# Attention scores of a hybrid decoder layer from split queries and keys, halves stacked over the 128 rows

## What is computed

```
qg = q.reshape(*lead, tq, N_KV_HEADS, GROUP, HEAD_DIM)
s = jnp.einsum('...qkgd,...skd->...kgqs', qg, k) * (HEAD_DIM ** -0.5)
s = jnp.where(valid, s + bias, -jnp.inf)
p = softmax of s with a sink logit per head
o = jnp.einsum('...kgqs,...skd->...qkgd', p, v)
...
z = h @ w_in        # queries, keys, values, gates, convolution inputs
y_conv = (cb * short_conv(u_ext, conv_w)) @ w_conv_out
mix = sigmoid(ga) * y_conv + sigmoid(gb) * (o @ w_attn_out)
x = x + mix @ w_o;  x = x + hier_moe(rms_norm(x))
```

## Time and profile before

| | us |
|---|---|
| median of 3 runs (lowest, highest) | 1737.24 (1736.86, 1740.86) |
| the profiled execution: its time | 1738.65 |
| its span from the first to the last instruction | 1737.1 |

### The profile page before, as it was taken

How to read it: one execution, slowest core, us unless ns; L and a number is a source line. 1 busy time by engine, 2 the same in 40 slices (tenths; PEclk the granted TensorE clock), 3 DMA queues, 4 the chain that set the end, 5 groups by cost and what they waited for, 6 DMA issues and landing times. The chain is left out here.

```text
span 1737.1 us, 26183 instructions
## 1 busy us (share of the span) xinstructions
PE 1653.6 (95%) x9527; PEld 1474.4 (85%) x9527; DVE 1036.5 (60%) x1839; ACT 834.0 (48%) x1202; POOL 234.0 (13%) x197
## 2 busy tenths in 40 slices
PE   5999999999999999999999999699999999999991
PEld 4899899999999999999999888478888888877871
DVE  5322466656556432114222576788989899888883
ACT  5000355555555430113112211378788888877773
POOL 1100000000000100000000111322322323222310
PEclk9999999999999999999999999799999999999996
DMA  6242111111111301114113711799999999999956
GB/s 161 79 125 86 40 41 46 49 36 36 36 49 48 101 25 49 49 36 158 41 44 120 255 73 72 266 379 375 379 375 372 381 370 380 373 368 367 365 206 218
DMA packets 131856, 305.30 MB, mean 176 GB/s; under 512 B 30403, under 2 KB 92079, under 8 KB 106935
## 3 DMA queue, kind: packets, MB, share of 16 engines
q1 hardware_dynamic: 115415, 267.76, 42.2%
q0 software_dynamic: 16384, 36.76, 7.3%
HBM read 282.81 MB, written 40.41 MB: 186 GB/s over the span
## 5 line engine op out<-in xcount | busy, mean ns | idle before, releaser
L1847 DVE TENSOR_TENSOR e_lo<-e_raw,e_hi 128x2048 fp32r<-128x2048 f32 x192 | 434.5, 2287 | 58.6 <-ACT e_hi L1332 34.1
L1332 ACT ACTIVATE e_hi<-e_raw 128x2048 fp32r<-128x2048 f32 x192 | 366.1, 1921 | 64.6 <-PE bank L1033 30.2
L1031 PE MATMUL bank<-e_hi,xT_hi 128*128 128x512 f32 x512 | 206.8, 404 | 6.7 <-DVE xT_lo L1852 6.7
L1127 ACT ACTIVATE w_hi<-w_raw 128x1024 fp32r<-128x1024 f32 x68 | 71.6, 1053 | 284.4 <-PE bank L704 252.8
L702 PE MATMUL bank<-h_hi,w_hi 128*128 128x344 f32 x624 | 202.8, 325 | 1.1 <-DVE h_lo L1452 1.1
L1033 PE MATMUL bank<-e_hi,xT_lo 128*128 128x512 f32 x512 | 202.5, 395 | 0.0
L1032 PE MATMUL bank<-e_lo,xT_hi 128*128 128x512 f32 x512 | 201.9, 394 | 0.0
L703 PE MATMUL bank<-h_lo,w_hi 128*128 128x344 f32 x624 | 199.9, 320 | 0.0
L704 PE MATMUL bank<-h_hi,w_lo 128*128 128x344 f32 x624 | 199.8, 320 | 0.0
L847 PE MATMUL bank<-h_hi,w_hi 128*128 128x344 f32 x576 | 197.3, 342 | 2.0 <-DVE w_lo L1433 2.0
L848 PE MATMUL bank<-h_lo,w_hi 128*128 128x344 f32 x576 | 184.8, 321 | 0.0
(11 more groups left out here) (327 smaller groups left out, 3134.6 us busy)
## 6 DMA issues: line engine op xcount, KB each, us to landing
e_raw<-in_w_e_gate_dram SPq DMA_DIRECT2D x64, 1024.0 KB
e_raw<-in_w_e_up_dram SPq DMA_DIRECT2D x64, 1024.0 KB
e_raw<-in_w_e_down_dram SPq DMA_DIRECT2D x64, 1024.0 KB
w_raw<-in_w_in_dram SPq DMA_DIRECT2D x104, 256.0 KB, 3.1
a_spill<-y_sb POOLq DMA_DIRECT2D x8, 516.0 KB, 2.9
a_raw<-a_spill SPq DMA_DIRECT2D x2, 2064.0 KB, 9.6
x_tok<-in_x_prompt_dram SPq DMA_DIRECT2D x4, 1024.0 KB, 10.7
w_raw<-in_w_attn_out_dram SPq DMA_DIRECT2D x32, 128.0 KB, 2.9
```

The source lines that it names most:

```text
L1031: pe.matmul(out, xT_hi[:, par, kk, :], wh, start=kk == 0, stop=False)
L1332: A.activation(e_hi[:, slot % 4, :], e_raw[slot][:, :], ACT.Copy).then_inc(e_hi_done, 1)
L1847: V.tensor_tensor(e_lo[slot][:, :], e_raw[slot][:, :], e_hi[:, slot % 4, :].bitcast(F32), ALU.subtract).then_inc(e_lo_done, 1)
```

## The change

The scores are made from split operands too. For each head the high half of the queries stands on 64 rows and the low half on the other 64 (`q_a` for the first head of a pair, `q_b` for the second). The keys' high half stands on both sets of rows (`kk_hi`), and so does their low half (`kk_lo`). One matmul over 128 rows of `q_a` by `kk_hi` gives high by high plus low by high, a second by `kk_lo` gives the other two terms. A pair of heads is so four fp32r matmuls.

The staging of a block is cut in two, t = 0 for pairs 0 to 3 and t = 1 for pairs 4 to 7. POOL writes the high halves of queries and keys on their own rows, ACT the keys' high half on the other rows (`twin`), DVE all low halves (`stage_low`). ACT and DVE do this in the middle of a step: part 1 of block j at i = 2, part 0 of block j + 1 at i = 5.

To make room, `w_lo` is laid over `w_raw`, slot for slot. A slot can be loaded again only when PE is done with the unit that used it, so SP waits for `chunk_done` where it waited for `lo_ready`, and the slots of the units in phases B and C are numbered otherwise.

```diff
-        q_stage = at("q_stage", R5, [KT, P])
-        k_stage = at("k_stage", R5 + 4096, [2, 2 * P])
+        q_a = at("q_a", R5, [KT, P], F32R)
+        q_b = at("q_b", RING + 24576, [KT, P], F32R)
+        kk_hi = at("kk_hi", RING + 28672, [KV, 2 * P], F32R)
+        kk_lo = at("kk_lo", RING + 32768, [KV, 2 * P], F32R)
...
-        w_lo = at("w_lo", RING + 24576, [3, KT, P], F32R)
+        w_lo = at("w_lo", RING, [3, KT, P], F32R)
...
-                    sp.wait_ge(lo_ready, wait)
+                    sp.wait_ge(chunk_done, wait)
...
-            def stage(b, first):
...
-                    pool.tensor_copy(k_stage[:, :, :], k_sb[:, :, bass.ds(b * P - P, 2 * P)]).then_inc(staged, 1)
-                pool.tensor_copy(q_stage[:, :, :], q_sb[:, :, bass.ds(b * P, P)]).then_inc(staged, 1)
+            def stage(b, t):
+
+                if not isinstance(b, int):
+                    pool.wait_ge(scores_ready, b * 8 + (4 * t - 4))
+                st = slice(4 * t, 4 * t + 4)
+                pool.tensor_copy(q_a[0:64, st, :], q_sb[0:64, st, bass.ds(b * P, P)])
+                pool.tensor_copy(q_b[64:128, st, :], q_sb[64:128, st, bass.ds(b * P, P)])
...
-                if st == 0:
-                    pe.wait_ge(staged, b * 2 + 2)
+                if st % 4 == 0:
+                    pe.wait_ge(staged, b * 2 + (t + 1))
+                    pe.wait_ge(twin_done, b * 2 + (TWIN_FROM + t + 1))
+                    pe.wait_ge(stage_lo, b * 2 + (STAGE_FROM + t + 1))
...
-                    mm = pe.matmul(SCB[h][:, place + off:place + 256], q_stage[64 * h:64 * h + 64, st, :],
-                                   k_stage[64 * h:64 * h + 64, t, off:256], start=True, stop=True)
+                    q2, out = (q_a, q_b)[h], SCB[h][:, place + off:place + 256]
+                    pe.matmul(out, q2[:, st, :], kk_hi[:, 2 * t + h, off:256], start=True, stop=False)
+                    mm = pe.matmul(out, q2[:, st, :], kk_lo[:, 2 * t + h, off:256], start=False, stop=True)
...
-            def split_hi(u, slot, uses, freed):
+            def split_hi(slot, uses):
...
-                if freed is not None:
-                    act.wait_ge(chunk_done, freed)
...
+            def twin(b, t, first=False):
+                if not first:
+                    act.wait_ge(scores_ready, b * 8 + (4 * t - 4))
...
+                A.activation(kk_hi[64:128, 2 * t, keys], k_sb[0:64, t, old], ACT.Copy)
+                A.activation(kk_hi[0:64, 2 * t + 1, keys], k_sb[64:128, t, old], ACT.Copy).then_inc(twin_done, 1)
...
+                    if i == 2 and not first:
+                        twin(j, 1)
+                    if i == 5 and not last:
+                        twin(j + 1, 0)
...
+            def stage_low(b, t, first=False):
+
+                dve.wait_ge(staged, b * 2 + (t + 1))
+                dve.wait_ge(twin_done, b * 2 + (TWIN_FROM + t + 1))
...
+                V.tensor_tensor(q_a[64:128, st, :], q_sb[0:64, st, now], q_a[0:64, st, :].bitcast(F32), ALU.subtract)
+                V.tensor_tensor(q_b[0:64, st, :], q_sb[64:128, st, now], q_b[64:128, st, :].bitcast(F32), ALU.subtract)
...
+                    for dst in (own, other):
+                        ins = V.tensor_tensor(kk_lo[dst, 2 * t + h, keys], k_sb[own, t, old], kk_hi[own, 2 * t + h, keys].bitcast(F32), ALU.subtract)
+                ins.then_inc(stage_lo, 1)
...
+                    if i == 2 and not first:
+                        stage_low(j, 1)
+                    if i == 5 and not last:
+                        stage_low(j + 1, 0)
```

More of the change, by code:

```diff
@@ L402, in q_unit @@
                 if wait is not None:
-                    sp.wait_ge(lo_ready, wait)
+                    sp.wait_ge(chunk_done, wait)
                 load(slot, [(w_raw[slot][:, :, 64 * h:64 * h + 64],
                              w_in_t[:, :, bass.ds(col[h], 64)]) for h in range(2)])
[L407 to L414, removed]
-            for v in range(2):
-                cols(v, w_in_t, COL_V // P + v, U_V + v - 1)
-            with sp.Fori(0, KT) as j:
+            for j in range(4):
+                q_unit(0, j, j % 3, 3 if j == 3 else None)
+            cols(1, w_in_t, COL_K // P, 6)
+            for j in range(4):
+                q_unit(1, j, j % 3, (12, 15, 15, 18)[j])
+            cols(1, w_in_t, COL_K // P + 1, 21)
+            for v in range(2):
+                cols(2 * v, w_in_t, COL_V // P + v, 27)
+            cols(1, w_in_t, COL_CC // P, 30)
+            for s, col in ((1, COL_CH), (2, COL_CB)):
+                cols((s + 1) % 3, w_in_t, col // P, 39)
+            with sp.Fori(1, KT) as j:
                 for s, col in enumerate((COL_CC, COL_CH, COL_CB)):
-                    cols(s, w_in_t, j + col // P, j * 3 + (U_B + s - 1))
+                    cols((s + 1) % 3, w_in_t, j + col // P, j * 9 + (33 + 3 * s))
             def out_cols(slot, col, wait):
-                sp.wait_ge(lo_ready, wait)
+                sp.wait_ge(chunk_done, wait)
                 for t, loaded in enumerate((raw_loaded[slot], ao_loaded[slot])):
@@ L559, in _ @@
             pool.wait_ge(bias_loaded, 16)
-            stage(0, True)
+            for t in range(2):
+                stage(0, t)
             flat = lambda x: x.rearrange("b s g d -> b s (g d)")
@@ L569, in _ @@
             with pool.Fori(0, KT - 1) as j:
-                stage(j + 1, False)
+                for t in range(2):
+                    stage(j + 1, t)
                 spill(j)
@@ L779, in _ @@
                     xh, xl = h_hi[:, k, P * n:P * n + rows], h_lo[:, k, P * n:P * n + rows]
-                    pe.matmul(out, xh, w_hi[:, 0:2, k, :], start=k == 0, stop=False)
-                    pe.matmul(out, xh, w_lo[:, 0:2, k, :], start=False, stop=False)
-                    mm = pe.matmul(out, xl, w_hi[:, 0:2, k, :], start=False, stop=k == KT - 1)
+                    pe.matmul(out, xh, w_hi[:, 0:3:2, k, :], start=k == 0, stop=False)
+                    pe.matmul(out, xh, w_lo[:, 0:3:2, k, :], start=False, stop=False)
+                    mm = pe.matmul(out, xl, w_hi[:, 0:3:2, k, :], start=False, stop=k == KT - 1)
                 mm.then_inc(chunk_done, 1)
@@ L1143, in _ @@
                 if g == 0:
[L1144 to L1158, removed]
+                    split_hi(0, 1)
+            for slot, uses in ((1, 1), (2, 1), (0, 2), (1, 2), (0, 3), (1, 3), (2, 2), (0, 4), (1, 4)):
+                split_hi(slot, uses)
+            split_hi(0, 5)
+            split_hi(2, 3)
+            split_hi(1, 5)
             def store_o(t, b):
@@ L1513, in invert_sums, with step_b @@
                 V.reciprocal(rden[:, pair], rden[:, pair]).then_inc(sums_inverted, 1)
-            def step_b(j, first):
+            def stage_low(b, t, first=False):
+                dve.wait_ge(staged, b * 2 + (t + 1))
+                dve.wait_ge(twin_done, b * 2 + (TWIN_FROM + t + 1))
+                st = slice(4 * t, 4 * t + 4)
+                now = slice(0, P) if first else bass.ds(b * P, P)
+                V.tensor_tensor(q_a[64:128, st, :], q_sb[0:64, st, now], q_a[0:64, st, :].bitcast(F32), ALU.subtract)
+                V.tensor_tensor(q_b[0:64, st, :], q_sb[64:128, st, now], q_b[64:128, st, :].bitcast(F32), ALU.subtract)
+                keys, old = (slice(P, 2 * P), slice(0, P)) if first else (slice(0, 2 * P), bass.ds(b * P - P, 2 * P))
+                for h in range(2):
+                    own, other = slice(64 * h, 64 * h + 64), slice(64 - 64 * h, 128 - 64 * h)
+                    for dst in (own, other):
+                        ins = V.tensor_tensor(kk_lo[dst, 2 * t + h, keys], k_sb[own, t, old], kk_hi[own, 2 * t + h, keys].bitcast(F32), ALU.subtract)
+                ins.then_inc(stage_lo, 1)
+            def step_b(j, first, last=False):
                 off = P if first else 0
@@ L1580, in step_b @@
                     if i % 3 == 0:
-                        split_lo(j * 3 + (U_B + i // 3 + 1), (i // 3 + 1) % 3)
+                        split_lo(j * 3 + (U_B + i // 3 + 1), (i // 3 + 2) % 3)
                 return step.n
+            stage_low(0, 0, True)
+            stage_low(0, 1, True)
             n0 = step.n
```

133 lines of the change are left out of this document (70 added, 63 removed).

## The result

The changed kernel takes 1765.83 us (median of 4 runs, 1762.72 to 1769.47), the kernel before 1738.52 us beside it: a ratio of 1.016, 95% interval 1.0145 to 1.0174, slower. I had said 1743 us, in a range of 1727 to 1754. The sign was right, the size was not: +27 us where I had summed +5. The sign was no strong call either, for I had given "slower" 0.53 and "the same" 0.27.

The account below looks back on a forecast made before the run. PE was taken to bound phase B, with DVE and ACT sharing one chain. Steps 1 to 6 +4.2, step 7 -0.8, step 0 -1.0, starts -1.1 and +1.8, slots +1.5 and +0.5: +5, so 1743 us, range 1727 to 1754.

Parts of the forecast that it names:

- What PE saves: Scores in phase B: four fp32r matmuls at 0.47 us replace a pair costing 0.81, saving 2.7 us a step.
- The walk through the step: Phase B chain of DVE and ACT: losses of 3.4 us against 2.7 saved, +0.7 us a step.
- scores(3) and values(1): Step at i = 2: the later maximum of pair 2 delays the low half of pair 1; PE loses 1.85 us.
- values(5): Step after i = 5: PE waits for the low half of pair 5, 0.65 us lost.
- restarts: PE starting again after its waits in a step: 0.1 us for each of three, 0.3 together.
- The end of the step: At i = 7, shorter POOL copies end before the convolution's lines, giving back 1.07 us; turning pair 7 still loses 0.5.
- The starts: V's first matmul 1.1 us earlier; phase B's start 1.8 us later, as scores(0) waits for weight and key low halves.
- The slots: Later weight loads mostly fit; two tight places cost 1.5 us (low halves of `o`) and 0.5 us (ACT's load wait).
- Rival 4: Weight loads show through the slots, 1 us for each of 30 units: 1773 us; chance 0.03.
- Rival 1: The DVE and ACT chain has 2.5 us more slack a step, so PE's saving reaches the end: 1720 us; chance 0.2.
- Rival 3: Stacked score matmuls cost 0.20 us each, so 2.7 us a step is not saved: 1750 us; chance 0.05.
- Rival 2: POOL's fp32r writes are slower or block DVE's small lines, so 1.07 us a step stays lost: 1749 us; chance 0.2.

Follow-up runs that it names:

- e6: From e4, subtractions in eight places a step where DVE waits longest, those of step 0 between the copies of V: 1721.68 us, ratio 0.9915.
- e3: Changed kernel with `stage_low` no longer waiting for ACT's two copies of the keys (`twin`): 1755.85 us, ratio 1.0108.
- e2: Changed kernel with the six subtractions replaced by one of two columns in steps after the first, so scores use old low halves: 1727.92 us, ratio 0.9946.
- e4: Changed kernel with the subtractions in four parts behind maximum and inverse of pairs 2, 3 and 4, 5, without the wait for `twin`: 1728.73 us, ratio 0.9952.
- e5: From e4, the six subtractions of part 1 together again ahead of the maximum of pair 2: 1746.86 us, ratio 1.0052.
- e7: From e6, low weight halves in phase C in a room of their own, so loads wait for the low half again: 1714.48 us, ratio 0.9872.
- e1: Changed kernel with the old scores, staging and order of phase B, keeping only the new weight slots: 1740.89 us, ratio 1.0016.

## Why the prediction was right in sign and wrong in size

**What PE saves: right.** 0.34 us a pair, 2.7 a step. Without the waits a step takes 47.20 us (e6), 49.95 - 47.20 = 2.75. The heads of a pair no longer stand on different 64 rows, and the pair still became shorter. The Trainium skill, "TensorE: Matmul & The Clock Gate", Part 3, says that matmuls on different row groups run at once, which spoke against giving this up. Here the new pair takes 0.48 us for four matmuls, the pitch of the values matmuls, against 0.81 for the old one.

**The walk through the step: it failed in size.** The losses were to be 3.4 us and are 53.01 - 47.20 = 5.8 us. Term by term:

| term | predicted | measured |
|---|---|---|
| `stage_low` itself | 2.5 | 3.10 |
| maximum of pair 2 later against scores(2) | 3.2 | 5.21 - 0.82 = 4.4 |
| scores(3) and values(1) | 1.85 | 1.72 + 0.94 = 2.66 |
| scores(6) | 0.1 | 0.63 |
| values(5) | 0.65 | 0.91 |
| turning of pair 7 | 0.5 | 0.47 |
| restarts | 0.3 for three | 5.8 - 4.67 = 1.1 for five (a remainder) |

The first step that failed is the price of `stage_low`. I took 0.60 us for 512 columns and 0.33 for 256 because rows ahead of another instruction overlapped it. Here 512 columns follow each other after 406.69 - 405.99 = 0.70 us and 256 columns after 1.72 / 4 = 0.43: no overlap at all. The second is an origin. I counted the twin and the maximum from scores(2) of before, but the new scores(2) comes 0.34 us earlier against ACT and DVE: ACT's scaling ended at 1.02 behind it and not at 0.54, the twin at 1.9 and not at 1.5, and DVE began at 2.05. e3 gives the price of the wait behind such a block, 0.7 us at each place. The two errors make the maximum of pair 2 1.2 us later than I had it; of this 0.8 shows in the waits ahead of scores(3) and values(1), and at pair 5 0.5 in that ahead of scores(6). The third is the restart: 410.50 to 410.73 is 0.23 us where the pair's next pitch is 0.11, and the loss of a step exceeds the listed waits by 1.1 us. I had 0.1 apiece; that it is all restart is argued from these rows, not shown by a run.

At values(5) I named the wrong releaser: the low half of pair 5. It is ACT's storing of the outputs (L1173), which stands at i = 6 behind the high half of that pair. It needed no mending of its own, for in e2, e4, e5 and e6 it is gone; in e3 it stands at 0.90.

**The end of the step: right.** POOL's relief came: the line of 8 columns has a median of 220 ns (the line ahead of it one of 1286), where they were 996 and 1570:

```profile
L1612 DVE SCALAR_TENSOR_TENSOR y_sb<-histT,cols,y_sb x8: 215/220/353, 228.8 to 594.7; 128x8 f32<-128x8 f32 x8
```

But the copies now meet other lines, as this one of DVE and this one of POOL:

```profile
435.27 0.61 DVE L1531 TENSOR_TENSOR rden<-den,esink 128x2 f32<-128x2 f32 x1 [1.26 <-ACT esink L1203]
```

```profile
435.26 0.61 POOL L560 CAST q_a<-q_sb 64x512 fp32r x1 [21.67 <-PE bank L814]
```

This line of 2 columns has a median of 161 ns; beside the copy it ends with it. By the section "Who interferes with whom" of the Trainium skill's page "SBUF — State Buffer" it should be blocked for the whole copy, and the trace agrees. POOL's four pieces took 2.55 us there (435.26 to 437.81), where I had estimated 1.8.

**The starts: missed by 1.4 us up to step 1, with luck in between.** V's first matmul came 1.15 us earlier (159.54 against 160.69, 1.1 predicted). The 1.8 us of B's start were the first unit's, forecast from 190.36 to 192.15, or with V's gain 0.7 us later than before; it started at 190.53, 0.2 later. That scores(0) stands 1.8 us later than before (189.64 against 187.83) is another quantity, and its likeness to my term is luck. What I left out is the clock, on both sides. At V's start PE waits 1.74 us and the granted clock in the 2.5 us behind it is 1.00, where it was 0.50 behind 3.13 us before; V itself takes 25.7 us instead of 27.1.

In step 0 the clock went the other way. e4 and e5 are the same program up to its end and both wait 4.37 us for scores(0), but the clock from 190 to 195 us was 0.66 in e4 and 0.50 in e5, and step 0 took 43.14 and 44.52 us; all of the difference lies between scores(0) and scores(1). The changed kernel, with 0.50 too, took 45.86: the 1.3 us more come behind its block at i = 5, with waits of PE of 0.50 us ahead of scores(6) and 0.51 at the last turning. I had priced neither.

**The slots: half failed.** Rival 4 (a load shown at each of 30 units) did not happen. But C grew by 7.3 us, where I took 1.5 and 0.5 us for its two tight places. On ACT the high half of the next weights stands between the high halves of `o`, and on DVE their low half stands ahead of all eight low halves of `o`:

```profile
663.30 1.06 ACT L1142 ACTIVATE w_hi<-w_raw 128x1024 fp32r<-128x1024 f32 x1 [3.08 <-DMA w_raw<-in_w_attn_out_dram]
```

```profile
664.39 1.23 DVE L1452 TENSOR_TENSOR w_lo<-w_raw,w_hi 128x1024 fp32r<-128x1024 f32 x1 [12.30 <-ACT w_hi L1142]
```

A load released later holds ACT for 3.08 us, and DVE begins the low halves of `o` at 665.53, 61.0 us behind the start of C, where it was 56.6 before. They come one each 1.14 us, and PE uses them faster: four waits of 0.36 to 0.41 us instead of one of 0.40, 1.2 us more, where I had taken 1.5. The second place failed: a row of four waits of 0.4 for `a_lo` and one of 1.0 behind them, 2.6 us against 0.5. And a third place I had not counted: `q_new` (1.2 us), which stands on DVE behind a low half of weights that waits for ACT. The listed waits make 5.0 us more than before; that the other 2.3 are slow first matmuls behind them is argued, not shown. e7 gives all of it back.

**Rivals and range.** Rival 1 (1720) is what the same work does when it is placed well (e4: 1728.7, e6: 1721.7), not what this order does. Rival 3 is refuted by the pair's 0.12 us a matmul. Rival 2's price did not come, for the 1.07 us are back; what it feared, a blocked line of DVE, did happen, to `rden` (0.61 us instead of 0.16 in the row above). No run takes that out of the changed order by itself: in e2 and e6 none of its 64 instances is over 0.16 us. The true case was my forecast's own mechanism with nearly every term larger: of 22 us missed, 14 lie in steps 1 to 6, 5 in C, and 1.4 and 1.3 ahead of step 1 and in step 7. The walk, "good to about 1 us a step", was off by 2.4, all to one side.

## What to carry to other kernels

When two engines hand one chain to and fro, put new work of either into its own waits for the other, behind the step that releases it: 3.1 us ahead of a maximum cost up to 2.4 us a step, the same 3.1 us in such waits cost nothing that shows (e6). In a walk, price instructions at their full length unless rows of the same pair of kinds overlap, and ask how much slack a place has before adding to it: 0.7 us ahead of a maximum cost at most 0.2 us a step alone (e2), and all of its 0.7 behind a block that had used the slack up (e3). Where a buffer is made to serve twice, look at what is queued behind the wait that moves, not only at whether the transfer fits.

## What the runs showed of the hardware that I had not expected

- The granted clock behind an idle stretch of PE at the start of phase B, in the window of 190 to 195 us: 1.00 behind waits of 1.2 us (e1) and 1.4 us (e6, e7), 0.66 behind 2.04 us (before). Behind 4.37 us it was 0.50, the lower level of 1.2 GHz, in the changed kernel and e5, but 0.66 in e4 and 0.73 in e3, and 0.66 behind 5.03 us in e2. So the length of the wait alone does not fix it, and two executions of the same code differed by 1.4 us in step 0 (e4, e5).
- Subtractions over 64 rows are not cheaper than over 128: 0.69 us for 512 columns, as the low half of the probabilities over 128 rows and as that of the values, which has both inputs in SBUF (L1593 of the changed kernel, 0.69), and 0.43 for 256, back to back.
- Four fp32r matmuls of 256 columns over all 128 rows took 0.48 us, less than four fp32 passes over 64 rows with what they disturb around them (0.81).
